# First modulation of a two-block transformer kernel: loaded and summed by blocks of 128 features, on one Trainium2 core

## What is computed

```python
mod = jax.nn.silu(c) @ w_ada[l] + b_ada[l]            # 1024 x 6144
shift1, scale1, gate1, shift2, scale2, gate2 = [m[:, None, :] for m in jnp.split(mod, 6, axis=-1)]
h = rms_norm(x, norm1_w[l]) * (1.0 + scale1) + shift1
proj = h @ w_in[l]
q, k, v, xBC, z, dt_raw, gates = jnp.split(proj, offsets, axis=-1)
dt = jax.nn.softplus(dt_raw.astype(jnp.float32).reshape(b, s, 2, N_SSD_HEADS) + dt_bias.astype(jnp.float32))
```

## Time and profile before

| what | value |
|---|---|
| times of the three runs shown, us | 1561.44, 1563.25, 1564.2 (median 1563.25) |
| span of the profiled execution, us | 1564.1 |
| TensorE busy, share of the span | 98% |
| VectorE, ScalarE, GpSimd busy | 73%, 53%, 58% |
| weight loads busy | 79% |
| TensorE share of the chain that ended last | 68% |
| bytes read from HBM, mean rate | 167.67 MB, 109 GB/s |
| first instruction of the step sizes' fold (L1617) | 44.35 us from the span's start |

### The profile page before, as it was taken

The page is one execution under the profiler, slowest core; times in us unless marked ns, Lnnn a source line. Parts: engine busy times, 40 slices in busy tenths (PEclk is TensorE's granted clock), DMA queues, the critical chain, the costliest instruction groups (busy, mean ns, idle before and its releaser), DMA issues.

```text
span 1564.1 us, 23063 instructions
## 1 busy us (share of the span) xinstructions
PE 1534.6 (98%) x7983; PEld 1238.5 (79%) x7983; DVE 1142.1 (73%) x1588; ACT 835.0 (53%) x1552; POOL 909.6 (58%) x644
## 2 busy tenths in 40 slices
PE   7999999999999999999999999999999999999998
PEld 4788888888878756687777888888888888888887
DVE  3798888888729888488459888778768895567542
ACT  3676766756734587423344444444558665454442
POOL 0556666666745776555846767777753467532314
PEclk8999999999999999999999999999999999999999
DMA  8444334434332310177622333333423334322212
GB/s 320 125 128 129 114 116 142 122 108 135 106 96 68 83 32 1 71 246 249 216 67 78 99 92 105 108 109 108 114 82 81 95 104 119 91 65 68 67 41 82
DMA packets 77484, 171.34 MB, mean 110 GB/s; under 512 B 8320, under 2 KB 10752, under 8 KB 73920
## 3 DMA queue, kind: packets, MB, share of 16 engines
q1 hardware_dynamic: 70064, 133.09, 29.0%
q10 hardware_dynamic: 7312, 36.83, 6.7%
HBM read 167.67 MB, written 2.23 MB: 109 GB/s over the span
## 4 chain that ended last, share of the span: by engine, by line
PE 68%; DVE 12%; issue 8%; POOL 5%; DMA 1%; ACT 1%; ACTq 0%; POOLq 0%; DVEq 0%; SPq 0%
PE bank L1401 8%; PE bank L1403 8%; PE bank L1419 8%; PE bank L1402 8%; PE bank L1422 8%; PE bank L1420 8%; PE bank L1864 5%; POOL w_lo L716 4%; PE bank L1866 3%; DVE ada_acc L2150 2%; DVE rstd L2449 2%; PE bank L1757 1%; PE bank L2016 1%; PE bank L1695 1%; DMA w_raw<-ws 1%
## 5 line engine op out<-in xcount | busy, mean ns | idle before, releaser
L716 POOL TENSOR_TENSOR w_lo<-w_raw,w_hi 128x512 fp32r<-128x512 f32 x442 | 648.7, 1492 | 405.0 <-ACT w_hi L775 404.6
L775 ACT ACTIVATE w_hi<-w_raw 128x512 fp32r<-128x512 f32 x444 | 260.2, 624 | 124.2 <-DMA w_raw<-ws 102.4
L1401 PE MATMUL bank<-a_hi_and_lo,w_hi 128*128 128x512 f32 (+1 forms) x808 | 319.0, 395 | 2.4 <-ACT gates_early L840 1.2
L1403 PE MATMUL bank<-a_hi_and_lo,w_lo 128*128 128x512 f32 (+1 forms) x808 | 311.8, 386 | 0.0
L1402 PE MATMUL bank<-a_hi_and_lo,w_hi 128*128 128x512 f32 (+1 forms) x808 | 311.4, 385 | 0.0
L1419 PE MATMUL bank<-b_hi,w_hi 128*128 128x512 f32 x536 | 210.2, 392 | 2.3 <-ACT tmp L1119 1.3
L1422 PE MATMUL bank<-b_lo,w_hi 128*128 128x512 f32 x536 | 209.3, 390 | 0.0
L1420 PE MATMUL bank<-b_hi,w_lo 128*128 128x512 f32 x536 | 209.0, 390 | 0.0
L1401 PEld LDWEIGHTS bank<-a_hi_and_lo,w_hi 128*128 128x128 f32 x808 | 151.9, 188 | 37.0 <-issue 4.4
L1402 PEld LDWEIGHTS bank<-a_hi_and_lo,w_hi 128*128 128x128 f32 x808 | 152.0, 188 | 31.1 <-issue 1.9
L1403 PEld LDWEIGHTS bank<-a_hi_and_lo,w_lo 128*128 128x128 f32 x808 | 151.7, 188 | 31.2
(11 more groups left out here) (441 smaller groups left out, 3182.7 us busy)
## 6 DMA issues: line engine op xcount, KB each, us to landing
w_raw<-ws SPq DMA_DIRECT2D x457, 256.0 KB, 2.7
cs_rows<-cs_scratch ACTq DMA_DIRECT2D x16, 1024.0 KB, 5.1
ada_piece<-ada ACTq DMA_DIRECT2D x16, 1024.0 KB, 5.7
ada_piece<-ada SPq DMA_DIRECT2D x8, 1024.0 KB, 17.2
x_stream<-x SPq DMA_DIRECT2D x2, 1024.0 KB, 8.9
x_stream<-x ACTq DMA_DIRECT2D x1, 2048.0 KB, 7.9
out<-x_stream SPq DMA_DIRECT2D x4, 256.0 KB, 2.8
out<-x_stream SPq DMA_DIRECT2D x8, 128.0 KB, 1.8
```

What stands on the lines that cost most here:

```text
L716: nc.gpsimd.tensor_tensor(wlo[b][:, :], full[:, :], r32(whi[b][:, :]), ALU.subtract)\
L775: A(whi[n % RING][:, :], full[:, :], ACT.Copy).then_inc(hi_done, 1)
L1401: mm(out, lh, rh, start=first, stop=False)
L1403: return mm(out, ll, rh, start=False, stop=last)
```

## The change

All eight pieces are now of one kind: piece k holds, for all 1024 features of `c`, the 128 shift columns and the 128 scale columns of feature block k. `sum_piece(k)` makes both as rows of 256, with the eight feature blocks of `c` spread over four partition groups, two in each; `turn_piece(k)` multiplies the copied rows by `pick`, a column that has a one in each group's first row, so that the groups are added and the rows turned in one step. VectorE makes gain and shift of block k from the two columns. The input block follows at once: blocks 0 to 3 are scaled on VectorE first (`scaled`), blocks 4 to 7 are only normed (`normed`), and ScalarE applies the gain with the bias. The step sizes' product of block k-2 stands behind the sum of piece k. The squares have eight buffers in place of two (`t0` to `t5`, `sq0`, `sq1`), and the root's table is loaded ahead of them. Slabs 0 and 1 are loaded behind pieces 0 and 4. `keep_clock` is 30 and 18 before the squares' sum, then 2 to 4.

```diff
@@ SyncE
-            for p in range(KT):
-                sp.dma_start(piece[p][:, :, :], d["ada"][p].rearrange("p (k n) -> p k n", k=2)).then_inc(ada_in[p], 16)
-                if p == KT // 2:
-                    sp.dma_start(raw[0][:, :], d["ws"][0]).then_inc(w_in[0], 16)
+            for k in range(KT):
+                sp.dma_start(piece[k][:, :, :], d["ada"][k].rearrange("p (k n) -> p k n", k=KT)).then_inc(ada_in[k], 16)
+                if k % (KT // 2) == 0:
+                    s = k // (KT // 2)
+                    sp.dma_start(raw[s][:, :], d["ws"][s]).then_inc(w_in[s], 16)
@@ ScalarE
+            A(small[:, 81:82], eps, ACT.Sqrt)
             for k in range(KT):
                 if k % (KT // 2) == 0:
                     act.wait_ge(s_x[k // (KT // 2)], 16)
-                square("n1", k, xF[:, k, :])
+                A(x_squares[k][:, :], xF[:, k, :], ACT.Square).then_inc(sq_ready, 1)
             root("n1", 1.0 / D_MODEL)
...
+            for k in range(KT):
+                act.wait_ge(mod_sum, k + 1)
+                A(mod_rows, MOD_ROWS[:, 0:2 * P], ACT.Copy).then_inc(mod_kept, 1)
+                if k % (KT // 2) == 0:
+                    hi_upto(k // (KT // 2))
+                act.wait_ge(mod1_ready, k + 1)
+                act.wait_ge(nfull, k + 1)
+                gain = 1.0 if k < SCALED_LATE else gain1[:, k:k + 1]
+                A(aH[:, k, :], xF[:, k, :], ACT.Identity, scale=gain, bias=modc[:, k:k + 1]).then_inc(hiA, 1)
@@ TensorE
+            def sum_piece(k):
...
+                pe.wait_ge(ada_in[k], 16)
+                if k:
+                    pe.wait_ge(mod_kept, k)
+                per = KT // SUM_GROUPS
+                for kk in range(per):
+                    for g in range(SUM_GROUPS):
+                        r, kb = slice(g * P // SUM_GROUPS, (g + 1) * P // SUM_GROUPS), g * per + kk
+                        ins = mm(MOD_ROWS[r, 0:2 * P], csl[:, kb:kb + 1].broadcast_to([P, P // SUM_GROUPS]),
+                                 piece[k][:, kb, :], start=(kk == 0), stop=(kk == per - 1))
                 ins.then_inc(mod_sum, 1)
+            def turn_piece(k):
+                pe.wait_ge(mod_kept, k + 1)
+                if k:
+                    pe.wait_ge(mod1_ready, k)
+                for half in range(2):
+                    ins = mm(MOD_COLS[:, 2 * k + half:2 * k + half + 1], mod_rows[:, half * P:(half + 1) * P], pick[:, :],
+                             start=True, stop=True)
                 ins.then_inc(mod_turned, 1)
+            def step_sizes():
+                k, (b, o) = next(dt_blocks)
+                pe.wait_ge(hiA, k + 1)
+                mm(gb(("dt",))[:, :], whi[b][:, o:o + P], in_a(k), start=(k == 0), stop=False)
+                pe.wait_ge(rdyA, k + 1)
+                return mm(gb(("dt",))[:, :], whi[b][:, o:o + P], in_a_lo(k), start=False, stop=(k == KT - 1))
...
+            keep_clock(spare, 30)
             pe.wait_ge(c_ready, 1)
+            pe.wait_ge(vec_prep, 2)
+            keep_clock(spare, 18)
             pe.wait_ge(n1_added, KT - 1)
             sum_squares(sq_sum, True, True).then_inc(stat_mm, 1)
+            keep_clock(spare, 4)
+            sum_piece(0)
             rows("n1")
+            keep_clock(spare, 3)
+            turn_piece(0)
+            for k in range(1, KT):
+                sum_piece(k)
+                if k > 1:
+                    step_sizes()
+                else:
+                    keep_clock(spare, 3)
+                turn_piece(k)
+                keep_clock(spare, 2)
+            step_sizes()
+            keep_clock(spare, 4)
+            step_sizes().then_inc(gemm_done, 1)
@@ VectorE
+            def columns(k):
+                ve.wait_ge(mod_turned, k + 1)
+                v(V.scalar_tensor_tensor(gain1[:, k:k + 1], MOD_COLS[:, 2 * k + 1:2 * k + 2], col("norm1", k), modc[:, KT + k:KT + k + 1],
+                                         ALU.mult, ALU.add))
+                V.tensor_tensor(modc[:, k:k + 1], MOD_COLS[:, 2 * k:2 * k + 1], col("bada", k), ALU.add).then_inc(mod1_ready, 1)
+                ve.wait_ge(mod1_ready, k + 1)
+                v.settle()
+            def normed(k):
+                V.tensor_tensor(xF[:, k, :], xF[:, k, :], PST[:, :], ALU.mult).then_inc(nfull, 1)
...
+            def full_a(k):
+                ve.wait_ge(nfull, k + 1)
+                v(V.tensor_scalar(t[k % 2][:, :], xF[:, k, :], gain1[:, k:k + 1], modc[:, k:k + 1], ALU.mult, ALU.add))
+                v.settle()
...
             wait_rows("n1")
+            for k in range(SCALED_LATE):
+                columns(k)
+                scaled(k)
+                if k:
+                    low_a(k - 1)
+            low_a(SCALED_LATE - 1)
+            for k in range(SCALED_LATE, KT):
+                normed(k)
+            for k in range(SCALED_LATE, KT):
+                columns(k)
+                full_a(k)
+                low_a(k)
```

More of the change, by code:

```diff
@@ L285 @@
 HALF_W = ADA_W // 2
-ROW_GROUPS = 4
 SUM_GROUPS = 4
[L288 to L291, removed]
+SCALED_LATE = 4
 SWAP = [i ^ 16 for i in range(32)]
@@ L411, in build @@
             with Arena():
-                piece = [sb(f"ada_piece{b}", [P, 2, HALF_W]) for b in range(KT)]
+                piece = [sb(f"ada_piece{b}", [P, KT, 2 * P]) for b in range(KT)]
             with Arena():
@@ L488, in build @@
         LEFT, RIGHT = slice(0, HALF_SEQ), slice(HALF_SEQ, SEQ)
[L489 to L493, removed]
+        MOD_ROWS, MOD_COLS = bank[3], bank[4]
+        mod_rows = std[:, 0:2 * P]
+        x_squares = [*t, *sq]
         HALF_SUMS, HALF_ROWS = (bank[2], bank[7]), (bank[2], bank[4])
@@ L1530, in turn_sums @@
                 ins.then_inc(ada_red, 1)
[L1532 to L1539, removed]
-                        ins = mm(SCALE_ROWS[r, 0:ROW_W], csl[:, k:k + 1].broadcast_to([P, P // ROW_GROUPS]),
-                                 piece[p][:, kk, j * ROW_W:(j + 1) * ROW_W], start=(k == 0), stop=(k == KT - 1))
-                if p == KT // 2 - 1:
-                    ins.then_inc(mod_sum, 1)
@@ L1545, in shift_part @@
-            def shift_part(q):
-                p = KT // 2 + q
-                pe.wait_ge(ada_in[p], 16)
-                if q >= 2:
-                    pe.wait_ge(mod_kept, q)
-                part = piece[p][:, :, :].rearrange("p h (k n) -> p (h k) n", n=PART_W)
-                for k in range(KT):
-                    for j in range(PART_KT):
-                        r = slice(j * P // PART_KT, (j + 1) * P // PART_KT)
-                        ins = mm(SHIFT_ROWS[q % 2][r, 0:P], csl[:, k:k + 1].broadcast_to([P, P // PART_KT]),
-                                 part[:, k, j * P:(j + 1) * P], start=(k == 0), stop=(k == KT - 1))
-                ins.then_inc(mod_sum, 1)
@@ L1581, in _ @@
+            sum_piece(0)
             rows("n1")
-            scale_piece(2)
-            keep_clock(gb(("dt",)), 5)
-            scale_piece(3)
-            keep_clock(gb(("dt",)), 3)
-            turn_scale()
-            keep_clock(gb(("dt",)), 3)
-            dt_blocks = enumerate(weights(("dt",)))
-            def dt_products(count):
-                for _ in range(count):
-                    k, (b, o) = next(dt_blocks)
-                    pe.wait_ge(rdyA, k + 1)
-                    mm(gb(("dt",))[:, :], whi[b][:, o:o + P], in_a(k), start=(k == 0), stop=False)
-                    ins = mm(gb(("dt",))[:, :], whi[b][:, o:o + P], in_a_lo(k), start=False, stop=(k == KT - 1))
-                return ins
@@ L2203, in low_a @@
             def low_a(k):
-                ve.wait_ge(nfull, k + 1)
                 ve.wait_ge(hiA, k + 1)
-                V.scalar_tensor_tensor(aL[:, k, :], xF[:, k, :], modc[:, k:k + 1], r32(aH[:, k, :]), ALU.add, ALU.subtract)\
-                    .then_inc(rdyA, 1)
-            scale_finish()
-            v(V.scalar_tensor_tensor(gain1, modc[:, KT:2 * KT], 1.0, col("norm1", 0, KT), ALU.add, ALU.mult))
-            v.settle()
-            wait_rows("n1")
-            for k in range(KT // 2):
-                scale_rows_of_x(k)
@@ L2215, in _ @@
[L2215 to L2228 removed]
+                if k < SCALED_LATE:
+                    ins = V.scalar_tensor_tensor(aL[:, k, :], xF[:, k, :], modc[:, k:k + 1], r32(aH[:, k, :]), ALU.add, ALU.subtract)
+                else:
+                    ins = V.tensor_tensor(aL[:, k, :], t[k % 2][:, :], r32(aH[:, k, :]), ALU.subtract)
```

96 lines of the change are left out of this document (13 added, 83 removed).

## The result

The changed kernel takes 1566.91 us (median of 20 runs, 1563.77 to 1572.74); before takes 1563.14 (20 runs, 1561.07 to 1565.93). The ratio is 1.0027, with a 95% interval of 1.0019 to 1.0034. The forecast of 1562.9 within 1560.6 to 1566.0 was wrong: the change costs some 4 us (3.8 by the two medians).

What follows compares the result with a forecast made beforehand. TensorE, busy 98% of the span, was taken as the bound, with only the front changing: 7.5 us gained at the first turn, given back by eight serial rounds, 43.3 - 43.7 = -0.4 us; predicted 1562.9, range 1560.6 to 1566.0.

Steps and rivals of the forecast that it cites:

- The first turn: Front of the program: block 0's turn on TensorE would start at 20.45 us, against 27.93 before.
- The round: Each of the first four blocks: turn, column operations, scaling, high part and copy all in a row, 2.77 us.
- The interval across the hole: Between blocks 3 and 4: four normings delay block 4's columns by 2.1 us, so one turn interval is about 4.2.
- TensorE's own pace: Last blocks, without the scaling on VectorE: TensorE's own work of 2.42 us a round sets the pace.
- The mark: Start of ScalarE's copy of the step sizes' sum: 43.3 us against 43.70, with everything behind it moving rigidly.
- full_a: Beside ScalarE's high part: from SBUF about half of 0.81 us, hidden wholly, moving the sum by at most 0.1.
- step one: Carrying the front's saving of 0.4 us to the whole: 1563.7 against the profiled span, 1562.9 against the runs' median.
- step two: Gap before the squares' sum, 1.4 us in place of 3.4: the granted clock was taken to hold through it.
- The rival: Low clock after TensorE idles 1.8 us at 34 to 36 us: costs 1.7 to 3.4, 1564.6 to 1566.3; chance 0.09.
- Slower by the low clock in the new gap: Clock falls near 17 us, at the idle before the squares' sum: 1568.4, or 1564.6 if recovering sooner; chance 0.12.
- Hand-overs shorter: In the rounds: TensorE sets the pace from the first round, a further -3.1 us, 1559.7; chance 0.07.
- The shift not reaching the end: Behind the front: a later wait on something the front does not move takes up the gain, 1563.25; chance 0.10.

Runs made afterwards that it cites:

- bridged: The kernel before with 45 clock-keeping products in place of 24 ahead of the scale's first piece, filling TensorE's gap; 1562.21 us, ratio 0.9998.
- again: The changed kernel run again with no edit, for its spread and a second trace; 1568.31 us, ratio 1.0037.
- look2: The changed kernel run a third time with no edit, for a further trace; 1567.49 us, ratio 1.0034.
- gapped: The changed kernel with 24 clock-keeping products in place of 48 ahead of the squares' sum, so TensorE idles there; 1569.21 us, ratio 1.0043.
- filled kinds: The changed kernel with added clock-keeping products: ahead of block 5's turn 1565.92 us, in the first round 1566.42, both plus five more elsewhere 1565.51.
- scaled8: The changed kernel with all eight blocks scaled first (SCALED_LATE 8 in place of 4); 1567.12 us, ratio 1.0035.
- ahead: scaled8 with the rows of block k+1 copied, into two buffers, before the high part of block k is written; 1563.53 us, ratio 1.0009.
- hole: The changed kernel with nine more clock-keeping products ahead of block 5's turn, where TensorE waits 1.6 us; 1565.92 us, ratio 1.0020.

## Why the prediction was wrong

**Right: the stage.** The first turn was forecast 15.65 us behind TensorE's start (20.45 from 4.80) and came at 14.0, since x's squares were all added at 15.94 in this execution and not at 16.78, and TensorE had started later. The round: 2.77 forecast, 2.85 measured, the columns' operations being a little longer. The interval across the hole: 4.2 and 4.22. TensorE's own pace: 2.42 and 2.46. The mark: 43.3 and 43.31. That these two agree to 0.01 is luck: the first turn came 0.8 sooner than forecast, the four rounds took 0.3 more, hole and last rounds 0.2 more, and from the last turn to the mark it was 3.15 in place of 2.8. (The end of the 48 products, 15.4 in the text, is 15.5 by its own terms, 11.69 + 3.84; nothing hangs on it.) `full_a` took 0.55 us, against the 0.81 of the PSUM row. The Trainium skill (VectorE: DVE Perf Modes, Mode 2x_2P) gives two results a cycle for it, and "about half" was worked out from that: it was shorter, but by a third and not by half. It is hidden beside the high part in either case. The pieces never were waited for, and what lies behind the mark shifted with it, to within 0.2 us up to the sums of squares 390 us later and to within 1.5 us up to the end (1520.4 us from mark to end before, 1518.9 now).

**Wrong, step one: "Against the profiled span this gives 1563.7; against the median of the runs, 0.85 below the span, 1562.9."** The saving of 0.4 us was worked out against one execution and then carried to the median. But the time of an execution lies above its span, by 1.7 to 2.1 us in all but one of those on record, where it is 2.5 (1564.0 for 1562.2, 1566.15 for 1564.4). So the profiled execution with its span of 1564.1 took about 1565.9, 2.8 above the median: it was one of the longest (the longest of the 20 has 1565.93), and a time had been set against a span. The text named the reason itself, "everything from the squares' sum at 18.86 to 24.2 ran at half speed", and then took that as before's state. `bridged` shows what the front of before is when the clock holds: a mark at 34.7 us from TensorE's start, not 38.9. "What the front gained (7.5 us at the first turn: half of it the clock...)" is therefore, for the half that is the clock, no gain at all for a typical execution. Against it the eight serial rounds stand uncovered: 3 to 4 us. In the forecast's own terms, its span of 1563.7 is a time of about 1565.5, 2.6 above the 1562.9 that was written, and the seven executions of the changed kernel at 0.998 have a median of 1565.9. That leaves 1.4 of the 4.0 us for step two.

**Wrong, step two: "I take it that the clock holds through it."** For the gap before the squares' sum this held in every trace of the changed kernel: it was 1.47 us in `again`, and in the result's trace and in `look2` the products reached up to the sum and there was none. For the hole it did not. The rival had the place, the mechanism and a price of 1.7 to 3.4 us; measured were 1.4 in `again` and 3.7 in `gapped`. Its chance of 0.09 was much too small: in three of the six traces with the open hole the clock fell behind it, and 9 of the changed kernel's 31 executions have a mean clock of 0.995 or less, wherever they lost it, against 3 of 86 before. The evidence against it, a wait of 1.8 us later in the program without a fall, was of the one profiled execution; and four other traces show a fall at about 440 us, in the stage that both kernels share, behind a wait of only 0.47 us. The length of a wait alone doesn't tell whether a fall follows.

**The sum.** Fixed part 3 to 4 us by the marks, 2.8 to 3.9 at the same mean clock. For the rest, the mean clock is 0.0013 lower, and before's own executions lose about 1 us for each 0.001 (1561.28 to 1565.28 from 0.999 to 0.995). Together some 4.1 to 5.3 us, and measured are 3.8 (result) to 5.1 (again). By the spans the fixed part looks smaller: `bridged` has 1560.5, the result's trace 1562.2 and look2's 1564.1, 1.7 and 3.6 more. The profiled executions of the changed kernel and its filled kinds are the first or second shortest of their runs, while bridged's is at its median, so these spans don't decide it. How the whole splits into the fixed part and falls is an estimate, and what share of an individual execution's time is due to which fall isn't shown: a trace exists of one execution of each run only, and the table's groups scatter by up to 5 us within themselves.

**The rivals.** Slower by the low clock in the new gap: `gapped` gives its price at the first turn (2.9 us), and no trace of the changed kernel shows it. Hand-overs shorter: no, the round was longer. The shift not reaching the end: no, it passes the sums of squares 390 us behind the mark whole, and a difference of 1.4 us comes only after them.

## What to carry to other kernels

A profiled execution is one draw. Before a saving is carried to a median, ask whether the stage it comes from was in its usual state in that draw; a granted clock of 0.50 for 10 us in a front of 40 is a warning, and the time to compare with is the same stage without it. And a pipeline by small blocks pays off only if no engine does two steps of neighbouring blocks in the wrong order: here one copy moved ahead of a high part took 3.6 us from the median (`scaled8` to `ahead`), about as much as the whole change had cost.

## What the runs showed that I had not expected

- The same wait of 1.60 us ahead of block 5's turn was followed by a fall in `again` and by none in the result's and look2's traces, with the same code.
- A fall lasted 3.4, 6.8 or 10.2 us. In gapped TensorE was busy for nearly all of its low stretch behind the hole, and the clock came back only at 51.10.
- The first landing of the constants varies from 4.8 to 6.8 us from the span's start. In look2, with 6.8, the mark came 1.2 us behind the result's; but between 4.86 (`hole`) and 5.63 (the result's) it didn't move the mark, 43.42 and 43.31. So "from TensorE's start" is a rough measure, good to about 1 us.
- The stage behind the front is rigid but not equal: from mark to end 1517.9 to 1520.4 us in the ten traces without a fall in it. Up to the sums of squares at some 434 us all 14 traces agree within 0.25 us, counted from the mark; of the 1.5 us between before and the changed kernel 0.1 lies ahead of them and the rest behind. Its cause wasn't looked for.
